# Modulation rows made in four places, and expert stages that begin on tile 0's routing

## The reference

```python
s_lat, s_ctx = silu(c), silu(c_ctx)
for layer in (0, 1):
    m_l = split(s_lat @ w_mod[layer] + b_mod[layer], 6)  # shift1 scale1 gate1
    m_c = split(s_ctx @ w_mod[layer] + b_mod[layer], 6)  # shift2 scale2 gate2
    z = concat(rms(xc)*(1+m_c[1]) + m_c[0], rms(xl)*(1+m_l[1]) + m_l[0])
    if layer == 0:                      # RWKV-7 heads beside an RG-LRU
        p = z @ even_w_in
        y = concat(rwkv7_mix(p[:, :1920]), rglru_mix(p[:, 1920:])) @ w_out
    else:                               # differential attention
        y = diff_attention(z @ w_qkv, ...) @ w_o   # latent queries only
    x = x + m[2] * y
    h = rms(x)*(1+m[4]) + m[3]
    # PEER: 8 heads, each scores 2x128 keys, takes 16 of 16384 experts
    x = x + m[5] * sum_over(head, k)( softmax(best) * gelu(u[e] . h) * v[e] )
return xl
```

## Time and profile before

| stage | from | to |
|---|---|---|
| modulation | 8 | 85 |
| normalise, layer 0 | 85 | 106.4 |
| project_even | 106.4 | 279.4 |
| rglru | 279.4 | 362.8 |
| rwkv_scan | 362.8 | 820 |
| rwkv_finish | 820 | 858 |
| experts, layer 0 (first gather at 912) | 858 | 2266 |
| normalise, layer 1 | 2266 | 2289 |
| attention_qkv | 2289 | 2438 |
| attention | 2438 | 2519 |
| experts, layer 1 (first gather at 2572) | 2519 | 3246 |

### The profile page before, as it was taken

One profiled execution on the slowest core, in us unless ns is written; L12 is line 12 of the kernel. 1 busy time (PEld: TensorE's weight loads), 2 busy tenths in 40 slices (PEclk: granted clock), 3 DMA queues, 4 the chain that ended last, 5 costly groups with the idle time before them and its releaser, 6 DMA issues. The chain is left out here.

```text
span 3252.5 us, 31375 instructions
## 1 busy us (share of the span) xinstructions
PE 2662.2 (82%) x9292; PEld 1311.6 (40%) x9292; DVE 2064.7 (63%) x4803; ACT 681.0 (21%) x1705; POOL 1061.9 (33%) x917
## 2 busy tenths in 40 slices
PE   5698699999589999777777777776897798887776
PEld 1343387878344444322222222222444344432222
DVE  1233533333567777888888888886146577778887
ACT  1114333323022121111111111112115112111111
POOL 0001332321124444444444444443000134344443
PEclk9899799999889999999999999999898899999999
DMA  8325300000359999999999999997300699999998
GB/s 337 101 74 229 135 1 1 1 2 1 131 218 406 395 402 409 400 420 420 416 420 420 420 418 420 420 420 320 141 17 4 257 419 420 420 419 414 421 421 332
DMA packets 136612, 930.68 MB, mean 286 GB/s; under 512 B 17196, under 2 KB 18220, under 8 KB 32580
## 3 DMA queue, kind: packets, MB, share of 16 engines
q0 software_dynamic: 111744, 805.46, 60.2%
q1 hardware_dynamic: 24776, 124.03, 10.1%
HBM read 928.28 MB, written 1.15 MB: 286 GB/s over the span
## 5 line engine op out<-in xcount | busy, mean ns | idle before, releaser
L1384 PE MATMUL psum<-ring,diag 128*128 128x512 f32 x3072 | 1493.5, 621 | 350.8 <-DVE diag L1503 349.7
L1262 POOL DMA_INDIRECT ring<-in_uv,experts x768 | 911.4, 1187 | 1478.7 <-PE psum L1384 1036.3
L1557 DVE CUSTOM_DVE_ANT_0 ring<-ring,hcur 128x1024 f32<-128x1024 f32 x768 | 941.3, 1226 | 301.9 <-DMA ring<-in_uv,experts 274.1
L1384 PEld LDWEIGHTS psum<-ring,diag 128*128 128x128 f32 x3072 | 557.2, 194 | 1198.0 <-DVE diag L1503 727.5
L1292 ACT ACTIVATE gel<-dots 128x1 f32<-128x1 f32 x768 | 148.4, 201 | 1415.8 <-DVE dots L1557 1414.4
L1503 DVE TENSOR_SCALAR diag<-ident,gel,wcur 128x128 f32<-128x128 f32 x768 | 257.9, 346 | 23.7 <-ACT gel L1292 23.7
L1027 DVE COPY_PREDICATED T<-level,psum 128x512 f32<-128x512 uint32 x80 | 58.7, 734 | 177.5 <-PE psum L810 177.5
L341 PE MATMUL psum<-zT,wring 128*128 128x512 f32 x368 | 161.1, 598 | 7.7 <-DMA wring<-in_w_in 7.7
L1621 PE MATMUL psum<-wring,zT 128*128 128x512 f32 x320 | 139.1, 598 | 10.5 <-DMA wring<-in_w_qkv 10.5
L1363 PE MATMUL psum<-yT,w_q 128*128 128x512 f32 (+1 forms) x256 | 120.6, 573 | 3.2 <-issue 3.2
L467 POOL DMA_DIRECT2D rows<-in_b_mod x24 | 11.9, 500 | 337.4 <-POOLq L88 279.5
(11 more groups left out here) (350 smaller groups left out, 2613.0 us busy)
## 6 DMA issues: line engine op xcount, KB each, us to landing
wring<-in_w_mod SPq DMA_DIRECT2D x12, 2048.0 KB, 12.6
wmod<-in_w_mod SPq DMA_DIRECT2D x24, 1024.0 KB, 8.9
w_q<-in_w_q SPq DMA_DIRECT2D x36, 512.0 KB, 7.9
ring<-in_uv,experts POOLq DMA_INDIRECT x768, 10.5
wring<-in_w_qkv SPq DMA_DIRECT2D x6, 2048.0 KB, 8.5
wring<-in_w_in SPq DMA_DIRECT2D x23, 512.0 KB, 3.7
bc<-modulation_rows SPq DMA_DIRECT2D x14, 512.0 KB, 6.9
w_all<-in_w_o SPq DMA_DIRECT2D x8, 512.0 KB, 6.4
```

Source lines behind the costliest of these rows:

```text
L1262: nc.gpsimd.indirect_dma_start(ring[:, s % RING], None, uv, bass.IndirectOffsetOnAxis(ap=experts[:, n, j:j + 1], axis=0)).then_inc(row_in[ ...
L1384: m = nc.tensor.matmul(ps[:, c], diag[:, j % DIAGS], ring[:, j % RING, D + 512 * c:D + 512 * c + 512], start=(first and j == 0), stop=(las ...
L1557: nc.vector.tensor_tensor_reduce(u, u, hcur[:], 1.0, 0.0, ALU.mult, ALU.add, dots[:, j:j + 1]).then_inc(dot_done, 1)
```

## The change

The modulation rows are made in four places instead of two. `modulation` makes four chunks (shift1 and scale1 of layer 0). `rglru` makes the other eight of layer 0, one after each unit, the last row after the fifth scan; the rows lie in a free part of `yT` and their stores are waited for by SP in `rwkv_scan`. `rwkv_finish` makes layer 1's first four chunks: SP loads eight halves of 1 MB behind its two arrays, PE sums them, ACT copies, POOL adds the bias and one, SP stores. The last eight chunks of layer 1 are made for the latent segment alone: in `attention_qkv` DVE sums 16 half chunks (`add_half`, four chained operations of 512 columns each) into `mod_acc`, from a ring of two slots that POOL's queue fills; at the places that `LATE_AT` names; `attention` sums over the partitions with eight matmuls by a column of ones among its transposes (now in 6 banks), and DVE adds bias. `normalise` is given `load_first`: SP issues the first five chunks of `w_in`, and the first three of `w_qkv`, behind the broadcast rows of the norm.

`out_and_experts` puts tile 0's routing ahead: PE turns tile 0 after one and a half projections, scores head 0 before head 1's queries, and makes the other projections after head 1's scores; the fourth one stands inside unit 0, which is written out apart from the loop, and the query parts of that unit start at its seventh row. DVE makes `out(1)` and `norm(1)`, then `out(2)` and `norm(2)`, before unit 0, and `out(3)` and `norm(3)` ahead of its ninth row.

```diff
-                for n in range(MOD_CHUNKS):
+                for n in range(FIRST_CHUNKS):
...
+                sp.wait_ge(row_done, FIRST_CHUNKS)
+                sp.dma_start(mod[0, :, 0:2 * D], row[:]).then_inc(rows_out, 16)
...
+LRU_CHUNKS = [(0, c) for c in range(FIRST_CHUNKS, MOD_CHUNKS)]
+LATE_CHUNKS = MOD_CHUNKS - FIRST_CHUNKS
...
-    return a["w_mod"][1, i // 2, :, GROUPS * (i % 2):GROUPS * (i % 2) + GROUPS]
+    layer, c = LRU_CHUNKS[i // 2]
+    return a["w_mod"][layer, c, :, GROUPS * (i % 2):GROUPS * (i % 2) + GROUPS]
...
-                for c in range(IN_CHUNKS):
-                    if c >= RING:
-                        sp.wait_ge(mm_done, c - RING + 1)
+                for c in range(RING, IN_CHUNKS):
+                    sp.wait_ge(mm_done, c - RING + 1)
...
-        MOD_AT = lambda u: range(u + (u > 0), u + 2 if u < 7 else MOD_CHUNKS)
+        MOD_AT = lambda u: range(u, u + 1)
...
+                for n in range(len(LRU_CHUNKS)):
+                    layer, c = LRU_CHUNKS[n]
                     pool.wait_ge(row_done, n + 1)
-                    pool.dma_start(mod[1, :, n * 512:(n + 1) * 512], row[:, n % 2]).then_inc(row_out[n % 2], 16)
-                for turn in range(2):
-                    pool.wait_ge(row_out[turn], 16 * (MOD_CHUNKS // 2))
+                    pool.dma_start(mod[layer, :, c * 512:(c + 1) * 512], row[:, n % SLOTS]).then_inc(row_out[n % SLOTS], 16)
+                    if n + SLOTS < len(LRU_CHUNKS):
+                        bias(n + SLOTS)
...
-                for n in MOD_AT(7):
-                    mod_row(n)
+                    if u == 4:
+                        for n in MOD_AT(7):
+                            mod_row(n)
...
+                for done in rows_out:
+                    sp.wait_ge(done, 16 * (len(LRU_CHUNKS) // len(rows_out)))
...
+                for i in range(HALVES):
+                    k0 = GROUPS * (i % 2)
+                    sp.dma_start(wmod[:, i], a["w_mod"][1, i // 2, :, k0:k0 + GROUPS]).then_inc(wmod_in[i], 16)
+                for seg in range(2):
+                    sp.dma_start(brow[seg:seg + 1], a["b_mod"][:, 1, 0:2 * D]).then_inc(b_in, 16)
+                sp.wait_ge(row_done, FIRST_CHUNKS)
+                sp.dma_start(mod[1, :, 0:2 * D], row_[:]).then_inc(rows_out, 16)
+                sp.wait_ge(rows_out, 16)
...
+                pool.wait_ge(b_in, 32)
+                rstep = Chain(pool, row_own)
+                for n in range(FIRST_CHUNKS):
+                    if plus_one(n):
+                        rstep(nc.gpsimd.tensor_scalar(brow[:, n], brow[:, n], plus_one(n), None, ALU.add))
+                for n in range(FIRST_CHUNKS):
+                    pool.wait_ge(rsum_done, n + 1)
+                    nc.gpsimd.tensor_tensor(row_[:, n], row_[:, n], brow[:, n], ALU.add).then_inc(row_done, 1)
...
+                pe.wait_ge(o_read, 1)
+                for n in range(FIRST_CHUNKS):
+                    if n >= 2:
+                        pe.wait_ge(acc_done, n - 1)
+                    for i in (2 * n, 2 * n + 1):
+                        pe.wait_ge(wmod_in[i], 16)
+                        groups(nc, ps[:, 4 + n % 2], scolz, wmod[:, i],
+                               range(GROUPS * (i % 2), GROUPS * (i % 2) + GROUPS)).then_inc(part_mm, 1)
+                    pe.wait_ge(acc_done, n + 1)
+                    if n >= 2:
+                        pe.wait_ge(rsum_done, n - 1)
+                    nc.tensor.matmul(ps[0:2, 6 + n % 2], sel[:], acc[:, n % 2], start=True, stop=True).then_inc(rsum_mm, 1)
+                pe.wait_ge(rsum_done, FIRST_CHUNKS)
...
+    FIRST_QUERY, FIRST_SCORE, FIRST_S_COPY = 6, (10, 14), (11, 15)
+    FIRST_PART = lambda j: ((j - FIRST_QUERY) // 4, (2 * ((j - FIRST_QUERY) % 4), 2 * ((j - FIRST_QUERY) % 4) + 2)) if FIRST_QUERY <= j < FIRST_QUERY + 8 else (None, None)
...
-                project(1)
+                project(1, 0, KD // 2)
                 turn(0)
...
+                    if head == 0:
+                        pe.wait_ge(k_in, 16)
...
-                    project(i)
-                    turn(i - 1)
-                turn(NT - 1)
-                pe.wait_ge(ev_done, 2 * NT)
-                unit(0, True, False, AHEAD)
+                project(1, KD // 2, KD)
+                if NT > 2:
+                    project(2)
+                turn(1)
+                for j in range(TOPK):
+                    if NT > 2 and j == 4:
+                        project(3)
+                        turn(2)
+                    if NT > 2 and j == FIRST_QUERY:
+                        turn(3)
+                    if j == FIRST_QUERY:
+                        pe.wait_ge(ev_done, 2 * NT)
+                    m, ks = FIRST_PART(j)
...
-                out(1)
-                norm(1)
                 dve.wait_ge(c_in, 16)
                 dve.wait_ge(table_done, 1)
                 dve.sem_clear(route_own)
                 first = Chain(dve, route_own)
                 for part in range(8):
                     route_part(first, 0, part)
-                for i in range(2, NT):
-                    out(i)
-                    norm(i)
+                out(1)
+                norm(1)
                 route_part(first, 0, 9)
+                if NT > 2:
+                    out(2)
+                    norm(2)
...
+                        if NT > 2 and isinstance(n, int) and n == 0 and j == EXP_AT:
+                            out(3)
+                            norm(3)
...
+                    if i == 0:
+                        unit(0, 0, 2 * AHEAD)
+                    with dve.Fori(1 if i == 0 else 0, HEADS - 1) as hd:
...
-    RING, G = 3, 2 * HEADS
-    GROUPS = (slice(0, 2), slice(2, 6))
+    RING, G, LATE_RING = QKV_RING, 2 * HEADS, 2
+    HALVES = 2 * LATE_CHUNKS
+    LATE_AT = (4, 5, 12, 12, 12, 12, HALVES)
...
+            @block.gpsimd
+            def _(pool):
+                for i in range(HALVES):
+                    if i >= LATE_RING:
+                        pool.wait_ge(half_done, i - LATE_RING + 1)
+                    k0 = GROUPS * (i % 2)
+                    pool.dma_start(wmod[:, i % LATE_RING], a["w_mod"][1, FIRST_CHUNKS + i // 2, :, k0:k0 + GROUPS]).then_inc(wmod_in[i % LATE_RING], 16)
...
+                def add_half(i):
+                    dve.wait_ge(wmod_in[i % LATE_RING], 16 * (i // LATE_RING + 1))
+                    sums = mod_acc[:, i // 2]
+                    for n in range(GROUPS):
+                        w, c = wmod[:, i % LATE_RING, n], scol[:, GROUPS * (i % 2) + n, 1:2]
+                        if i % 2 == 0 and n == 0:
+                            out = nc.vector.tensor_scalar(sums, w, c, None, ALU.mult)
+                        else:
+                            out = nc.vector.scalar_tensor_tensor(sums, w, c, sums, ALU.mult, ALU.add)
+                        if n < GROUPS - 1:
+                            step(out)
+                    out.then_inc(half_done, 1)
+                    dve.wait_ge(half_done, i + 1)
+                for i in range(LATE_AT[0]):
+                    add_half(i)
...
+                    for n in range(LATE_AT[i], LATE_AT[i + 1]):
+                        add_half(n)
...
+                def late(n):
+                    if n >= 2:
+                        pe.wait_ge(late_done, n - 1)
+                    nc.tensor.matmul(ps[0:2, 6 + n % 2], ones[:], mod_acc[:, n], start=True, stop=True).then_inc(late_mm, 1)
+                pe.wait_ge(ones_done, 1)
                 for g in range(12):
-                    if g >= 8:
-                        pe.wait_ge(tr_done, g - 7)
+                    if g >= 6:
+                        pe.wait_ge(tr_done, g - 5)
+                    if g >= 4:
+                        late(g - 4)
...
+                sp.dma_start(late_b[:], a["b_mod"][:, 1:2, 2 * D:]).then_inc(lb_in, 16)
+                sp.wait_ge(late_done, LATE_CHUNKS)
+                sp.dma_start(mod[1, 1:2, 2 * D:], late_row[:]).then_inc(late_out, 16)
+                sp.wait_ge(late_out, 16)
...
+                        def load_first(sp):
+                            for c in range(IN_RING):
+                                sp.dma_start(wring[:, c], a["w_in"][c]).then_inc(w_in[c], 16)
...
```

201 lines of the change are left out of this document (129 added, 72 removed).

## The result

The changed kernel takes 3224.4 us (median of 6 runs, 3222.1 to 3233.3) where the kernel before takes 3259.3 beside it (3248.5 to 3268.2): a ratio of 0.990 (0.988 to 0.993), about 1% faster. The forecast was 3204, with a range of 3180 to 3224: the change did what was forecast nearly everywhere, and some 17 us were lost in the scan, where it changes no instruction of a computing engine (SP alone waits there for some stores).

What follows compares the result with a forecast made beforehand. It took each stage to have its own bound: DMA in layer 0's experts and modulation, TensorE in layer 1's projections, no engine in the recurrent stage. Eight terms summed to -50.6, so 3254.9 became 3204 us, range 3180 to 3224.

Steps and rivals of the forecast that it cites:

- The rival on the clock: Layer 0's expert units: PE's new idle time leaves its clock at 1.2 GHz, slower than before; chance 0.02.
- Modulation: Modulation stage: 4 chunks in place of 12 save eight load steps, -39.1 us (38 to 41 saved).
- First projection: Layer 0's first projection: first weights loaded during normalising let PE start earlier, -7 us (-6 to -8).
- recurrent stage: Recurrent stage: 8 chunks in place of 12, gates earlier and no wait for stores, -16.8 us (-11 to -17.5).
- Finish stage: Finish stage: layer 1's four chunks mostly hidden, POOL's last operations and store end it, +3 us (0 to +6).
- Layer 1's projections: Layer 1's projections: PE saves 8.9 us but DVE's 16 half chunks end the stage, -1 us (-9 to +13).
- Attention: Attention: eight rows' last sums among the transposes, with 6 banks in place of 8, +4 us (0 to +7).
- Layer 0's experts: Layer 0's expert stage: gathers start 9.4 us earlier, but the fourth projection inside unit 0 costs more, +12 (-9 to +17).
- Layer 1's experts: Layer 1's expert stage: first gather 9.4 us earlier, less 3.7 for gate and w_q loads among gathers, -5.7 (-9.4 to 0).

Runs made afterwards that it cites:

- b_again: The kernel before, run again unchanged, ten executions: six of 3249.6 to 3255.6 us, one of 3260.2, three of 3270.9 to 3274.8.
- s_proj: Changed kernel with scan start 1.8 us later, and the fourth projection and turns of tiles 2 and 3 ahead of unit 0: 3199.8 us, ratio 0.983.

## Why the prediction was wrong, step by step

**The step that failed is the sum's silence on the scan stage.** No term stood for the 457 us between the recurrent and the finish stage, since no instruction in them changed. The time of an unchanged stage was taken for fixed, though its clock is not: 17.2 us of a missing 18.8 (50.6 - 31.8) are there. The other stages together gave -49.0 for -50.6, which is nearer than their terms were and so in part luck: 5.0 more at the modulation hide 3.3 less at layer 1's experts and 2.2 less at its projections. The rival on the clock looked at idle time that the change itself makes, in layer 0's units, and was right that it costs little there (the clock is 0.97 over the units' stretch); it didn't ask whether the clock can be lost at a light place that was there all along. The kernel before had that risk in the open: three runs spread over 20 us (3248.5 to 3268.2), and the forecast took their median as the kernel's one time, where another level lay 0.4 to 0.8% above it (3265 to 3278).

*Modulation*, -44.1 for -39.1. The eight chunks' 39.1 held. The rest was at the edges: the fourth chunk came at 33.97, not 36.08, the last sum ran at the higher clock, and 3.3 passed from the last row's start to the next stage's first load, where it was 4.6. Part of the 5 lies in the executions profiled: from its own first load the stage took 75.4 in the first trace and 72.7 in b_again. By the table's measure it is 82.4 to 85.1 in four traces before and 40.4 to 43.6 in ten after, some -41 in the mean.

*First projection*, -6.5, and *recurrent stage*, -15.4: both within the bounds given.

*Finish stage*, +3.5 for +3 (in six later traces the stage took 38.5 to 38.7, +1; in three it was as here). A small operation of DVE, POOL's last four operations, and two of DVE's passes beside its six:

```profile
777.50 4.11 DVE L1155 TENSOR_SCALAR st<-st 128x32 f32<-128x32 f32 x1
...
802.36 8.06 POOL L1142 TENSOR_TENSOR row__7<-row__7,brow 2x512 f32<-2x512 f32 x4
...
800.96 2.58 DVE L1170 TENSOR_TENSOR O<-O,rows 128x2048 f32<-128x2048 f32 x1
...
803.58 3.23 DVE L1171 TENSOR_TENSOR O<-O,KT 128x2048 f32<-128x2048 f32 x1
```

POOL's operations took 2.0 each, not the 1.1 forecast, and DVE's passes 2.58 (twice) and 3.23, each of which was 2.29 in the kernel before. So POOL's end is what ends the stage, as forecast, and the two engines held each other up. By the exclusion that the Trainium skill states ("SBUF — State Buffer", Who interferes with whom) the stage would end some 5 later, as the forecast estimated; the trace agrees in kind, since both engines lose, and less in size (3.5, or 1). The first row looks like a whole exclusion: DVE's operation on 32 columns took 4.11, where its like took 0.18 in the kernel before, and ended at 781.6, as POOL's product beside it did (777.07 + 4.50). It took 3.7 to 4.3, ending with the product, in the three later traces at 41, and 0.18 in the six at 38.6, where it stood just ahead of the product: that parts +3.5 from +1. Why the small operations at the end cost less than by the rule, no run took apart.

*Layer 1's projections*, +1.2 for -1, by the mechanism forecast. DVE in the changed kernel: its squares' mean, the root's wait, the last of seven halves, and the last sum.

```profile
2289.21 0.18 DVE L1774 TENSOR_SCALAR ss<-ss 128x32 f32<-128x32 f32 x1
...
2311.67 0.35 DVE L1776 RECIPROCAL ss<-ss 128x32 f32<-128x32 f32 x1 [22.28 <-ACT ss L1740]
...
2355.88 3.11 DVE L1757 SCALAR_TENSOR_TENSOR mod_acc<-wmod,scol,mod_acc 128x512 f32<-128x512 f32 x4 [2.93 <-DMA wmod<-in_w_mod]
...
2400.75 3.11 DVE L1757 SCALAR_TENSOR_TENSOR mod_acc<-wmod,scol,mod_acc 128x512 f32<-128x512 f32 x4 [0.28 <-DMA wmod<-in_w_mod]
```

DVE was past the seven halves at 2359.0, 105 into the stage (forecast 103.3), a pair costing 8.9 to 9.3 (forecast 8.6), and ended at 2403.9, ten us after PE (2393.3). Moving five halves into the wait of 22.28 took off 10 to 12.

*Attention*, +4.2 for +4. Later traces scatter more than the term is large: 84.9 to 86.6 in most with the change, 90 in two, 77.6 to 81.7 without it.

*Layer 0's experts*, +10.6 for +12. PE in unit 0, answering to the earlier trace rows: the first rows, the fourth projection (21 of its records; each of its 16 matmuls leaves two), the rows behind it, the first query, and unit 1's first row.

```profile
886.53 10.00 PE L1525 MATMUL psum<-ring,diag 128*128 128x512 f32 x16 [13.40 <-DVE diag L1592]
...
896.36 9.18 PE L1468 MATMUL psum<-scores,yT 128*128 128x512 f32 x21
...
910.97 3.60 PE L1525 MATMUL psum<-ring,diag 128*128 128x512 f32 x8
...
923.36 3.44 PE L1436 MATMUL psum<-yT,w_q 128*128 128x512 f32 x4 [3.82 <-issue]
...
959.97 1.98 PE L1457 MATMUL psum<-ring,diag 128*128 128x512 f32 x4 [0.48 <-DVE diag L1592]
```

POOL's gathers: the first, the ninth, and the two that had long waits.

```profile
857.11 1.09 POOL L1323 DMA_INDIRECT ring<-in_uv,experts  x1 [46.70 <-DVE experts L1582]
...
890.59 1.54 POOL L1323 DMA_INDIRECT ring<-in_uv,experts  x1 [22.98 <-PE psum L1525]
...
913.13 0.94 POOL L1323 DMA_INDIRECT ring<-in_uv,experts  x1 [14.95 <-PE psum L1525]
...
928.79 0.94 POOL L1323 DMA_INDIRECT ring<-in_uv,experts  x1 [13.01 <-PE psum L1525]
```

Unit 1's first row before, and a window of the changed kernel ahead of the gather at 913.13:

```profile
994.98 1.98 PE L1384 MATMUL psum<-ring,diag 128*128 128x512 f32 x4 [0.58 <-DVE diag L1503]
...
905.00:913.00 8.00, 8.00 (x26) 4.00 (x25) 2.51 (x3) 1.14 (x3) 0.00 (x0) 1.00 0.00 0
```

In stage time the first gather stands at 44.0 (forecast 44.7), the ninth at 77.5, PE's first query at 110.2 (forecast 110.6), unit 1 at 146.8 (forecast 146.6). Before, unit 1 began at 994.98, 137.0 into its stage: the change makes it 9.9 later, which is the whole loss but 0.7. The forecast had 992.6 there, since it left out one query and a short wait; the 2.4 are why its 12 came out as 9.9. The two holes in the transfers that were forecast are there: ahead of the ninth gather, and from 904 to 913, a DMA share of 0.00, while POOL waits 14.95 for rows that stand behind the projection. The wait of 13.01, for rows behind tile 3's norm and the reload, leaves a third one of some 4 us. In s_proj, the first rows, the first query and unit 1's first row:

```profile
882.37 7.09 PE L1524 MATMUL psum<-ring,diag 128*128 128x512 f32 x12 [4.11 <-DVE diag L1591]
...
898.66 1.88 PE L1436 MATMUL psum<-yT,w_q 128*128 128x512 f32 x4
...
933.72 1.98 PE L1457 MATMUL psum<-ring,diag 128*128 128x512 f32 x4 [0.49 <-DVE diag L1591]
```

DVE's first product came at 81.3, 4.3 earlier than in the kernel before, but the unit's first query still stands at its seventh row, at 103.6, and unit 1 began at 138.6: rows that come early with PE half idle buy nothing if the queries wait. That is read from the trace, not tried.

*Layer 1's experts*, -2.4 for -5.7. Its first gather, the ninth, and its first product:

```profile
2535.09 0.99 POOL L1323 DMA_INDIRECT ring<-in_uv,experts  x1 [139.31 <-DVE experts L1582]
...
2554.46 0.99 POOL L1323 DMA_INDIRECT ring<-in_uv,experts  x1 [8.03 <-PE psum L1525]
...
2544.40 1.22 DVE L1649 CUSTOM_DVE_ANT_0 ring<-ring,hcur 128x1024 f32<-128x1024 f32 x1
```

The gather is at 44.9 in its stage, 7.7 earlier than the earlier trace rows had it (52.7), not 9.4. The second tile's output and norm now stand on DVE between routing and product, so the product came only 4.0 earlier (54.3 for 58.2), and the ninth gather 5.7. The term took the whole lead of the gather, less the gate's loads, and left out what stands behind the gather on DVE, which it had counted for layer 0. Over nine traces with the new order the stage took 723.5 to 726.1, over five with the old one 727.9 to 730.3: some -4.4, nearer to the forecast than this pair.


## What to carry to other kernels

Before summing a change, list the stages behind it in which TensorE's work has short waits, and look at their granted clock in more than one execution; if the runs of the kernel spread by more than a few us, find out what the levels are, since a change may only move the kernel from one to the other. Where such a stage has a wait of a microsecond on every round, fill it with matmuls into a free bank that end before the wait does, and look at the other light places again. Work moved inside a pipelined loop costs what the loop's transfers lose while it runs, and that isn't given back where the rest of the stage is bound by the same transfers.
